# First attention: bias from skewed row slices, head norms inside the value projection, plain fp32 scores

## The chip, the cores and the metric

One core of a Trainium2 chip runs the kernel, one launch for the whole computation. The metric is the time of that launch on the device in microseconds (us). The engines are named as in the profile: PE (TensorE, matmuls), PEld (its weight loads), DVE (VectorE), ACT (ScalarE), POOL (GpSimd), SP (SyncE, which here only issues DMAs). Each runs its own instruction stream in program order and waits for the others by semaphores.

## What is computed

Two transformer blocks on 512 tokens of width 1024, in fp32. The change touches the first attention alone: 8 heads of width 64 whose queries and keys are normalised per head, with a bias that depends only on the distance of query and key, clipped at 128, and a mask by chunks of 64.

```python
def chunked_attention(q, k, v, q_gain, k_gain, rel_bias):
    q = rmsnorm(q.reshape(B, S, N_HEADS, HEAD_DIM), q_gain)
    k = rmsnorm(k.reshape(B, S, N_HEADS, HEAD_DIM), k_gain)
    ...
    rel_idx = jnp.clip(qpos - kpos, -REL_CLIP, REL_CLIP) + REL_CLIP
    bias = rel_bias.astype(jnp.float32)[:, rel_idx]
    ...
        s = jnp.einsum('bqhd,bkhd->bhqk', qb, kb).astype(jnp.float32) * scale + bias
        s = jnp.where(valid[None, None], s, NEG_INF)
        p = jax.nn.softmax(s, axis=-1)
        return jnp.einsum('bhqk,bkhd->bqhd', p.astype(vb.dtype), vb)

def hybrid_mixer(h, w_in, q_gain, k_gain, rel_bias, pool_w, pool_scale, w_out):
    proj = h @ w_in          # q, k, v, u: 512 columns each
    a = chunked_attention(q, k, v, q_gain, k_gain, rel_bias)
    p = multiscale_pool(u, pool_w, pool_scale)
    return jnp.concatenate([a, p], axis=-1) @ w_out
```

## The kernel before

Activations lie transposed (128 features on the partitions, 512 tokens along the row). A precise product is made of three products of the faster type fp32r, high by high, high by low and low by high part (`split3`, lines 357, 360, 361), so each weight block is cast by ACT (`split_hi`, L603) and its remainder taken by DVE (`split_lo`, L1123). SP fetches weight blocks of 512 KB into a ring of 4; a block's place is free when PE starts the block three ahead of it, and ACT and DVE prepare blocks 2 ahead of the one in use. Every engine's order is written out by hand.

The mixer of the first block runs as follows. `columns("qk", 8, ...)` makes eight tiles of queries and keys (head pair i in tile i); ACT squares each (`head_sq`), and `head_stat` sums the squares per head (L1985). `values("v", ...)` makes the value projection, k = 0 to 7, 12 products each; between them stand `head_stat` for the last pairs, `turn_rstd` (L1993, the inverse norms turned to rows) and `head_spread` (L2018, a row spread over 64 partitions). On the other side ACT takes the square root (L744) and casts the rows (L747), DVE takes the reciprocal (L1288) and the rows' remainder (L1290), then scales each tile (`qk_full`, L1302); ACT casts the result (L752) and DVE takes its remainder (L1294). Then `side_steps("u", ...)` makes the first tile of u.

The attention goes in 18 steps w; p = w // 4 is the head pair, q = w % 4 the query tile, so a step handles 128 queries against 128(q+1) keys for two heads c, called units 2w and 2w+1. In a step PE makes the scores (`a_scores`, units in partitions 0 to 63 and 64 to 127, output in banks 4 and 5), weighs values of a pair begun 5 steps ago (`a_weigh`, L2067), turns the probabilities of the step before (`a_turn`, L2080) and fills in products of u. DVE adds the bias and takes the minimum (`a_min`, L1319), and at w = 4, 9 and 14 empties a tile of u (`u_tile`, L1363), without which the next tile's products can't start; `pooled_lo` (L1358) stands ahead of it at w = 8. ACT takes the exponential (L770) and the copies L779 and L791.

The near part of the bias (where distance is not clipped, 192 or 256 columns) is made per head: ACT issues a DMA that reads the padded row from DRAM at 128 shifts (`toeplitz`, L726), PE multiplies it with a reversal matrix (`a_bias`, L2043 and L2044, bank 2), and ACT copies it out (L758, L759). Two heads are made before step 0, one each in steps 2, 3, 6, 7, 10 and 11. The order in which they stand there:

```python
            pe.wait_ge(acc_free, RES["v"] + TT)
            for h in range(2):
                a_bias(h)
            pe.wait_ge(qk_lo, 8)
```

## Time and profile before

| what | value |
|---|---|
| median of 3 runs | 1593.04 us |
| the three runs | 1593.31, 1587.33, 1593.04 us |
| profiled execution, own time | 1593.06 us |
| its span, first to last instruction | 1591.3 us |
| mean granted TensorE clock | 0.991 |
| PE busy | 1551.6 us (98%) |
| DVE, ACT, POOL busy | 760.0, 573.1, 79.1 us |
| chain that ended last | PE 90%, DVE 4%, ACT 2% |

The profile is of one execution. A row in order of time gives start, length, engine, line, operation, output<-input and in brackets how long the engine stood idle and who released it. Matmul lengths overlap, so what a matmul costs is read from the distance of two starts. In a row of a stretch, PEclk is the granted TensorE clock (1.00 is 2.4 GHz, 0.50 is 1.2 GHz).

### The profile page before, as it was taken

How to read it: one execution, taken by the hardware profiler on the slowest of the kernel's cores; microseconds unless marked ns; L12 is line 12 of the kernel's file. 1: busy time of each engine (PE TensorE's matmuls, PEld its weight loads, DVE VectorE, ACT ScalarE, POOL GpSimd, SP SyncE). 2: the span in 40 equal slices, each digit the busy share in tenths (PEclk: the TensorE clock that was granted, in tenths of full speed). 3: DMA queues.
4: the chain of work that ended last, by engine and by line, in shares of the span. 5: the costliest groups of instructions: out<-in, count | busy, mean ns of one | idle time of the engine just before them, and what ended most of it. 6: DMA issues, size and time to landing. Idle time of an engine off the chain costs nothing.

```text
span 1591.3 us, 19192 instructions
## 1 busy us (share of the span) xinstructions
PE 1551.6 (98%) x7150; PEld 1257.2 (79%) x7150; DVE 760.0 (48%) x1104; ACT 573.1 (36%) x941; POOL 79.1 (5%) x66
## 2 busy tenths in 40 slices
PE   8999999999989899999999999999998999999998
PEld 7888888878866688888888878777777888888886
DVE  5444422456365554444323465686644543244434
ACT  5222221234236442322212363446643343124322
POOL 0000000001013110000000051100000000000000
PEclk9999999999999999999999999999999999999999
DMA  6333333333221233333333333321131332233322
GB/s 189 95 92 100 98 94 97 101 101 110 78 63 41 66 106 93 97 100 92 97 102 93 96 103 90 110 80 41 49 137 41 93 93 105 93 93 92 102 97 93
DMA packets 246026, 147.66 MB, mean 93 GB/s; under 512 B 17472, under 2 KB 230096, under 8 KB 245840
## 3 DMA queue, kind: packets, MB, share of 16 engines
q1 hardware_dynamic: 232896, 141.58, 29.8%
q10 hardware_dynamic: 13072, 5.31, 1.3%
q8 instruction: 37, 0.61, 0.2%
q14 instruction: 21, 0.17, 0.0%
HBM read 142.66 MB, written 4.21 MB: 92 GB/s over the span
## 4 chain that ended last, share of the span: by engine, by line
PE 90%; DVE 4%; ACT 2%; issue 1%; DMA 1%; POOL 0%; SPq 0%; DVEq 0%; ACTq 0%; POOLq 0%
PE bank L357 29%; PE bank L361 28%; PE bank L360 28%; DVE w_low L1123 1%; ACT w_high L603 1%; PE bank L2266 1%; PE bank L2067 1%; PE bank L2383 1%; PE bank L2080 1%; DMA region_f<-in_x 0%; PE bank L1985 0%; DVE c_acc L1508 0%; DMA w_raw<-in_w_out 0%; DVE d_s L1489 0%; PE bank L2171 0%
## 5 line engine op out<-in xcount | busy, mean ns | idle before, releaser
L357 PE MATMUL bank<-region,w_high 128*128 128x512 f32 (+1 forms) x1484 | 586.1, 395 | 7.5 <-DVE region L1178 1.4
L361 PE MATMUL bank<-region,w_low 128*128 128x512 f32 (+1 forms) x1484 | 579.1, 390 | 0.0
L360 PE MATMUL bank<-region,w_high 128*128 128x512 f32 (+1 forms) x1484 | 579.1, 390 | 0.0
L1123 DVE TENSOR_TENSOR w_low<-w_raw,w_high 128x1024 fp32r<-128x1024 f32 (+1 forms) x259 | 335.7, 1303 | 147.8 <-ACT w_high L603 143.8
L603 ACT CAST w_high<-w_raw 128x1024 fp32r<-128x1024 f32 (+1 forms) x259 | 265.4, 1027 | 259.1 <-DMA w_raw<-in_ffn_w_down 106.9
L357 PEld LDWEIGHTS bank<-region,w_high 128*128 128x128 f32 (+1 forms) x1484 | 278.9, 188 | 71.1 <-DVE w_low L1123 5.9
L361 PEld LDWEIGHTS bank<-region,w_low 128*128 128x128 f32 (+1 forms) x1484 | 278.8, 188 | 60.2
L360 PEld LDWEIGHTS bank<-region,w_high 128*128 128x128 f32 (+1 forms) x1484 | 279.0, 188 | 57.6
L357 PE MATMUL bank<-w_high,region 128*128 128x512 f32 x416 | 166.1, 399 | 4.5 <-DVE w_low L1123 1.8
L361 PE MATMUL bank<-w_high,region 128*128 128x512 f32 x416 | 163.5, 393 | 0.0
L360 PE MATMUL bank<-w_low,region 128*128 128x512 f32 x416 | 163.4, 393 | 0.0
L657 ACT CAST region<-ff_t 128x512 f32 (+1 forms) x76 | 47.2, 621 | 207.1 <-DVE ff_t L1169 203.4
L1166 DVE TENSOR_TENSOR ff_u<-bank,rstd 128x512 f32<-128x512 f32 x44 | 30.4, 692 | 152.0 <-PE bank L361 152.0
L357 PEld LDWEIGHTS bank<-w_high,region 128*128 128x128 f32 x416 | 79.0, 190 | 23.1 <-DVE w_low L1123 2.7
L361 PEld LDWEIGHTS bank<-w_high,region 128*128 128x128 f32 x416 | 78.9, 190 | 17.0
L360 PEld LDWEIGHTS bank<-w_low,region 128*128 128x128 f32 x416 | 79.0, 190 | 15.7
L1178 DVE TENSOR_TENSOR region<-ff_t,region 128x512 f32 (+1 forms) x76 | 52.3, 688 | 52.0 <-ACT region L657 52.0
L1163 DVE TENSOR_TENSOR ff_z<-bank,rstd 128x512 f32<-128x512 f32 x44 | 30.4, 691 | 97.8 <-PE bank L361 89.7
L1199 DVE SCALAR_TENSOR_TENSOR x<-bank,x 128x512 f32<-128x512 f32 x24 | 16.6, 690 | 125.7 <-PE bank L361 125.6
L646 ACT ACTIVATE ff_s<-ff_z 128x512 f32<-128x512 f32 x44 | 27.9, 634 | 125.4 <-DVE ff_z L1163 125.3
L655 ACT ACTIVATE ff_t<-ff_z 128x512 f32<-128x512 f32 x32 | 20.3, 633 | 107.3 <-DVE ff_z L1176 107.3
L357 PE MATMUL bank<-f_rest,w_high 128*128 128x512 f32 x128 | 51.0, 399 | 0.0
(259 smaller groups left out, 1171.1 us busy)
## 6 DMA issues: line engine op xcount, KB each, us to landing
w_raw<-in_ffn_w_down SPq DMA_DIRECT2D x48, 512.0 KB, 4.0
w_raw<-in_ffn_w_gate SPq DMA_DIRECT2D x44, 512.0 KB, 3.7
w_raw<-in_ffn_w_up SPq DMA_DIRECT2D x44, 512.0 KB, 3.7
w_raw<-in_w_in SPq DMA_DIRECT2D x40, 512.0 KB, 3.8
w_raw<-in_w_up SPq DMA_DIRECT2D x32, 512.0 KB, 3.9
w_raw<-in_w_down SPq DMA_DIRECT2D x32, 512.0 KB, 3.2
w_raw<-in_w_out SPq DMA_DIRECT2D x16, 512.0 KB, 3.7
region_f<-in_x SPq DMA_DIRECT2D x4, 512.0 KB, 7.3
```

The costliest lines, as they stand in the source:

```text
L357: mm = pe.matmul(out, a_hi, b_hi, start=start, stop=False)
L360: pe.matmul(out, a_hi, b_lo, start=False, stop=False)
L361: return pe.matmul(out, a_lo, b_hi, start=False, stop=stop)
L603: last = act.copy(piece(w_high[b % RING]), piece(w_raw[b % RING]))
L646: act.activation(ff_s[:, j % 2, :], ff_z[:, j % 2, :], ACT.Silu).then_inc(s_ready, 1)
L655: act.activation(ff_t[:, j % 2, :], ff_z[:, j % 2, :], ACT.Square).then_inc(t_ready, 1)
L657: act.copy(dst[:, bass.ds(idx, 1), :] if it is not None else dst[:, idx, :], ff_t[:, j % 2, :]).then_inc(hid_hi, 1)
L1123: last = dve.tensor_tensor(piece(w_low[b % RING]), piece(w_raw[b % RING]), piece(w_high[b % RING]).bitcast(F32), ALU.subtract)
L1163: dve.tensor_tensor(ff_z[:, j % 2, :], bank[r % BANKS][:], rstd[:], ALU.mult).then_inc(z_ready, 1)
L1166: dve.tensor_tensor(ff_u[:, j % 2, :], bank[(r + 1) % BANKS][:], rstd[:], ALU.mult).then_inc(acc_free, 2)
L1178: dve.tensor_tensor(low_of(dst, place, idx, it), ff_t[:, j % 2, :], place.bitcast(F32), ALU.subtract).then_inc(hid_done, 1)
L1199: dve.scalar_tensor_tensor(x[:, n, :], acc[:], 0.5, x[:, n, :], ALU.mult, ALU.add).then_inc(acc_free, 1)
```

## The change

The near bias is no longer computed on PE. DVE writes the padded row reversed and negated (`rel_back`), ACT stores it to DRAM and copies all eight heads' rows 128 times over (`rel_rep_dram`, 128 x 12 KB) in the first FFN; `bias_load` then reads for each head two skewed slices (64 rows of 192 and of 256 elements) straight into `bias`, for heads 0 to 3 before the mixer, for 4 and 5 in step 4, for 6 and 7 in step 8. The constant parts of `bias` are set by DVE in the first FFN. The head norms' statistics, square root, turn and rows stand earlier in the value projection, among the weight blocks' casts. The scaled queries and keys stay fp32 (`over[1]`, the same memory as `part[1]`), without cast and remainder, and the scores are one fp32 matmul per unit.

```diff
@@ buffers
-        toep = sb("toep", [P, 2, 2, P])
-        rel_rows = sb("rel_rows", [HEADS, 384])
+        rel_rows = sb("rel_rows", [HEADS, N_REL])
+        rel_back = sb("rel_back", [HEADS, REL_ROW])
...
+        rel_rep_dram = nc.dram_tensor("rel_repeated_rows", [P, HEADS * REL_ROW], F32).ap()
@@ ACT: small loads in the first FFN, n is the tile of f1_dn0
                 if n == 0:
                     act.wait_ge(rel_padded, 1)
-                    act.dma_start(rel_pad_dram, rel_rows[:]).then_inc(rel_stored, 16)
+                    act.dma_start(rel_pad_dram, rel_back[:]).then_inc(rel_stored, 16)
+                if n == 1:
+                    act.wait_ge(rel_stored, 16)
+                    one = rel_pad_dram[0:1, 0:1].copy()
+                    act.dma_start(rel_rep_dram, bass.AP(one.tensor, one.offset, [[0, P], [1, HEADS * REL_ROW]])).then_inc(rel_repeated, 16)
@@ ACT: after the first FFN
-            act.wait_ge(rel_stored, 16)
-            for h in range(2):
-                toeplitz(h)
+            def bias_load(h):
+
+                if h >= 4:
+                    act.wait_ge(a_biased, 2 * TT * (h // 2 - 1))
+                for row0, width in ((0, 192), (64, 256)):
+                    at = REL_ROW * h + P - 1 - row0
+                    first = rel_rep_dram[row0:row0 + 1, at:at + 1].copy()
+                    skew = bass.AP(first.tensor, first.offset, [[HEADS * REL_ROW - 1, 64], [1, width]])
+                    act.dma_start(bias[row0:row0 + 64, h % 4, 256:256 + width], skew).then_inc(bias_in[h % 4], 16)
+            act.wait_ge(rel_repeated, 16)
+            act.wait_ge(bias_cleared, 1)
+            for h in range(4):
+                bias_load(h)
             act.wait_ge(lam_summed, 1)
             act.activation(lam_ex[:], bank[5][:, 0:2], ACT.Exp).then_inc(ev_hi, 1)
-            act.copy(head_select[:], const[:, C_HROW:C_HROW + 2 * S]).then_inc(select_made, 1)
             for i in range(8):
                 split_hi(BLK["qk"] + i + AHEAD)
                 if i == 0:
                     head("m1")()
+                if i == 3:
+                    act.copy(head_select[:], const[:, C_HROW:C_HROW + 2 * S]).then_inc(select_made, 1)
...
-            for i in range(3):
-                split_hi(BLK["v"] + i + AHEAD)
+            split_hi(BLK["v"] + AHEAD)
             act.wait_ge(h_stat, 8)
             act.activation(head_std[:], bank[4][:, 0:TT * 2 * HEADS], ACT.Sqrt, scale=1.0 / 64, bias=eps_col[:]).then_inc(h_std, 1)
+            split_hi(BLK["v"] + 1 + AHEAD)
             act.wait_ge(h_turned, 1)
             act.wait_ge(select_made, 2)
             act.copy(head_rows[0:2 * HEADS, :], bank[5][0:2 * HEADS, :]).then_inc(h_rows_hi, 1)
...
+            split_hi(BLK["v"] + 2 + AHEAD)
+            split_hi(BLK["v"] + 3 + AHEAD)
@@ ACT: step w of the attention
-                if w < 2:
-                    toeplitz(w + 2)
-                if q >= 2 and 2 * p + q < HEADS:
-                    bias_copy(2 * p + q)
-                    if 2 * p + q + 2 < HEADS:
-                        toeplitz(2 * p + q + 2)
+                if w in (4, 8):
+                    for h in (2 * p + 2, 2 * p + 3):
+                        bias_load(h)
@@ DVE: first FFN (pad_rows)
+                for s_ in range(4):
+                    link(dve.memset(bias[0:64, s_, 448:512], BIG))
+                    ins = dve.memset(bias[:, s_, 0:256], 0.0)
+                ins.then_inc(bias_cleared, 1)
@@ DVE: value projection
             for i in range(8):
-                if i == 2:
-                    split_lo(BLK["v"] + 3 + AHEAD)
+                if i in (2, 4):
+                    split_lo(BLK["v"] + 1 + i // 2 + AHEAD)
                 dve.wait_ge(h_bc, i + 1)
-                if i >= 2:
-                    dve.wait_ge(qk_lo, i - 1)
-                dve.scalar_tensor_tensor(qk_full[:, i % 2, :], qk_raw[:, i, :], qk_gain[:, i // 4:i // 4 + 1],
+                dve.scalar_tensor_tensor(over[1][:, i, :], qk_raw[:, i, :], qk_gain[:, i // 4:i // 4 + 1],
                                          bank[6 + i % 2][:], ALU.mult, ALU.mult).then_inc(qk_full_ready, 1)
-                if i > 0:
-                    qk_norm_lo(i - 1)
@@ DVE: a_min_of and the start of the attention
-                    dve.wait_ge(b_done, h + 1)
+                    dve.wait_ge(bias_in[h % 4], 32 * (h // 4 + 1))
...
-            for s_ in range(4):
-                link(dve.memset(bias[:, s_, 0:256], 0.0))
-                link(dve.memset(bias[0:64, s_, 448:512], BIG))
@@ PE
             def after_v(k):
-                if k == 1:
-                    for i in range(5, 8):
-                        head_stat(i)
+                for i in ((5,), (6, 7), (), (), (), (), (), ())[k]:
+                    head_stat(i)
+                if k == 2:
+                    turn_rstd(bank[5], 2 * HEADS, h_rec, h_turned)
                 if k == 3:
-                    turn_rstd(bank[5], 2 * HEADS, h_rec, h_turned)
                     pe.wait_ge(h_rows_lo, 1)
-                for i in ((), (), (), (0, 1), (2, 3), (4,), (5, 6), (7,))[k]:
+                for i in ((), (), (), (0, 1), (2, 3), (4, 5), (6, 7), ())[k]:
                     head_spread(i)
...
-                    split3(pe, bank[4 + c][:, 0:n], part[1][rows_, p, q * P:(q + 1) * P], part[1][rows_, 8 + p, q * P:(q + 1) * P],
-                           part[1][rows_, 4 + p, 0:n], part[1][rows_, 12 + p, 0:n], True, True).then_inc(a_score, 1)
+                    pe.matmul(bank[4 + c][:, 0:n], over[1][rows_, p, q * P:(q + 1) * P], over[1][rows_, 4 + p, 0:n],
+                              start=True, stop=True).then_inc(a_score, 1)
...
             pe.wait_ge(acc_free, RES["v"] + TT)
-            for h in range(2):
-                a_bias(h)
-            pe.wait_ge(qk_lo, 8)
+            pe.wait_ge(qk_full_ready, 8)
...
-                if q >= 2 and 2 * p + q < HEADS:
-                    a_bias(2 * p + q)
```

Where the instructions stand now. On PE in the value projection, the end of k=1 to the first spread, before:

```order
L1985 MATMUL bank<-const,head_sq 128x2 x12
...
L361 MATMUL bank<-w_high,region 128x512
L1993 MATMUL bank<-const,head_rstd 16x128 x4
L2018 MATMUL bank<-head_rows,head_select 128x512 x2
L357 MATMUL bank<-w_high,region 128x512
```

and of the changed kernel:

```order
L1970 MATMUL bank<-const,head_sq 128x2 x4
...
L1970 MATMUL bank<-const,head_sq 128x2 x8
...
L1978 MATMUL bank<-const,head_rstd 16x128 x4
L357 MATMUL bank<-w_high,region 128x512
...
L2003 MATMUL bank<-head_rows,head_select 128x512 x2
L357 MATMUL bank<-w_high,region 128x512
```

The turn (L1993, now L1978) and the first spread (L2018, now L2003) stood side by side and now have the 12 products of k=3 between them. On ACT in the same stretch, from the last square to the rows, before:

```order
L740 ACTIVATE head_sq<-region_f 128x512
L603 CAST w_high<-w_raw 128x1024 x3
L744 ACTIVATE head_std<-bank,eps_col 128x64
L747 CAST head_rows<-bank 16x512
L752 CAST region<-qk_full 128x512 x2
```

and of the changed kernel:

```order
L748 ACTIVATE head_sq<-region_f 128x512
L607 CAST w_high<-w_raw 128x1024
L751 ACTIVATE head_std<-bank,eps_col 128x64
L607 CAST w_high<-w_raw 128x1024
L755 CAST head_rows<-bank 16x512
L607 CAST w_high<-w_raw 128x1024 x2
```

Two of the three casts moved behind the square root, one of them behind the rows. On ACT in step 8 (its exponentials of 128 columns, the copy of turned probabilities, the cast of a pooled tile), before:

```order
L770 ACTIVATE a_p,a_sum<-a_s,a_min 128x128
L779 COPY region_f<-bank 128x4x128
L770 ACTIVATE a_p,a_sum<-a_s,a_min 128x128
L791 CAST region<-u_pad 128x512
L603 CAST w_high<-w_raw 128x512
```

and of the changed kernel:

```order
L764 ACTIVATE a_p,a_sum<-a_s,a_min 128x128
L773 COPY region_f<-bank 128x4x128
L764 ACTIVATE a_p,a_sum<-a_s,a_min 128x128
L732 DMA bias<-rel_repeated_rows 64x192
L732 DMA bias<-rel_repeated_rows 64x256
L732 DMA bias<-rel_repeated_rows 64x192
L732 DMA bias<-rel_repeated_rows 64x256
L785 CAST region<-u_pad 128x512
L607 CAST w_high<-w_raw 128x512
```

Four DMA issues now stand ahead of the cast of the pooled tile.

## Rows read from the trace of the kernel before

**Rows 1.** The page: its head and the busy time of TensorE (us, share, instructions).
```profile
span 1591.3 us, 19192 instructions
...
PE 1551.6 (98%) x7150; PEld 1257.2 (79%) x7150; DVE 760.0 (48%) x1104; ACT 573.1 (36%) x941; POOL 79.1 (5%) x66
```

**Rows 2.** PE in order of time, value projection (start, us, engine, line, op).
```profile
440.50 0.39 PE L361 MATMUL bank<-w_high,region 128*128 128x512 f32 x1
442.28 0.60 PE L1993 MATMUL bank<-const,head_rstd 128*16 128x128 f32 x4 [1.40 <-DVE head_rstd L1288]
444.27 1.22 PE L2018 MATMUL bank<-head_rows,head_select 128*128 128x512 f32 x2 [1.38 <-DVE head_rows L1290]
...
460.07 0.40 PE L357 MATMUL bank<-region,w_high 128*128 128x512 f32 x1
```

**Rows 3.** Chain that ended last, 432 to 446 us (start, us, what).
```profile
435.66 3.77 DMA w_raw<-in_w_in
...
439.45 1.06 ACT w_high L603
...
440.54 1.22 DVE w_low L1123
```

**Rows 4.** By stretches (length, PE, PEld, DVE, ACT, POOL, PEclk, DMA, GB/s).
```profile
446.00:448.00 2.00, 2.00 (x6) 1.52 (x6) 1.20 (x2) 1.12 (x2) 0.00 (x0) 0.50 0.35 99
```

**Rows 5.** In order of time, opening of the first attention: PE, then DVE, then ACT.
```profile
465.52 0.38 PE L2043 MATMUL bank<-const,toep 128*128 128x128 f32 x2
...
467.67 0.33 PE L357 MATMUL bank<-region 64*128 64x128 f32 x2
...
468.16 0.50 PE L357 MATMUL bank<-region,w_high 128*128 128x512 f32 x1
...
465.72 0.69 DVE L1363 TENSOR_TENSOR u_pad<-bank,rstd 128x512 f32<-128x512 f32 x1 [0.69 <-PE bank L361]
...
468.49 1.28 ACT L770 ACT_TABLE_LOAD   x1
```

**Rows 6.** PE in order of time, step 2 and the start of step 3.
```profile
473.59 0.39 PE L2043 MATMUL bank<-const,toep 128*128 128x128 f32 x2
...
473.96 0.47 PE L357 MATMUL bank<-region,w_high 128*128 128x512 f32 x1
...
475.98 0.50 PE L357 MATMUL bank<-region 64*128 64x512 f32 x1 [0.39 <-DVE a_min L1319]
```

**Rows 7.** PE in order of time, steps 7 and 8: scores, weighing (L2067), turns (L2080).
```profile
491.43 0.50 PE L357 MATMUL bank<-region 64*128 64x512 f32 x2
...
492.33 0.65 PE L2067 MATMUL bank<-region_f 128*64 128x256 f32 x4
492.92 0.87 PE L2080 MATMUL bank<-const,a_p 128*128 128x128 f32 x6
...
494.87 0.34 PE L357 MATMUL bank<-region 64*128 64x128 f32 x2
...
495.35 0.44 PE L2067 MATMUL bank<-region_f 128*64 128x128 f32 x4
495.72 1.09 PE L2080 MATMUL bank<-const,a_p 128*128 128x128 f32 x8
```

**Rows 8.** In order of time, steps 8 and 9: ACT, DVE, PE; then the issues of toep.
```profile
497.29 0.61 ACT L791 CAST region<-u_pad 128x512 fp32r<-128x512 f32 x1
...
499.14 0.68 DVE L1363 TENSOR_TENSOR u_pad<-bank,rstd 128x512 f32<-128x512 f32 x1
...
499.97 0.47 PE L357 MATMUL bank<-region,w_high 128*128 128x512 f32 x1 [0.53 <-DVE u_pad L1363]
...
L726 ACTq DMA_DIRECT2D toep<-rel_padded_rows x8: 326/326/574, 377.4 to 494.3; - x8
```

**Rows 9.** The page's DMA issues (KB each, median us to landing).
```profile
w_raw<-in_ffn_w_down SPq DMA_DIRECT2D x48, 512.0 KB, 4.0
...
x<-x_spill ACTq DMA_DIRECT2D x4, 512.0 KB, 5.6
```

64 lines of the change are left out of this document (16 added, 48 removed).

## The prediction

> **What bounds the kernel now.** I read the page first, then the chain of work that ended last, then TensorE's instructions in order of time wherever that chain leaves TensorE. The page says that PE is busy for 98% of the span [rows 1]: a microsecond is worth a microsecond only where PE stands still, runs at a lower clock, or does work that can go. The change touches four stretches: the value projection (about 427 to 460 us), the opening of the first attention (460 to 468), its 18 steps (to 530), and some DMA and VectorE work in the first FFN.
>
> In the value projection the reader is to see two standstills. The third product group's last product starts at 440.50; products follow each other every 0.227 us (24 of them between 460.07 and 465.52 [rows 2, 5]), so the next piece of PE work could start at 440.73. It starts at 442.28 (turning the inverse norms, which waited for the reciprocal), and the piece after it, the spread, at 444.27, after another 1.38 us of waiting [rows 2]. Who was late is in the chain: the cast L603 waited for a weight block whose DMA took until 439.45, and the square root, the reciprocal and the row split stand behind this cast and its remainder on their engines, though nothing in them needs that block [rows 3]. After the two standstills the granted clock is 0.50 of full, i.e. 1.2 GHz instead of 2.4, here for 446 to 448 us [rows 4].
>
> At the opening, the last weight product before the attention is followed at 465.52 by bias products; the first scores start at 467.67 and the next weight product at 468.16 [rows 5]. Between lie four bias products, two ACT evictions, and a wait for them.
>
> **The change, part by part.** The sum is made against the profiled execution: 1593.06 us, of which the span is 1591.3 [rows 1] and 1.76 lies outside; the median of the three runs is 1593.04, so both can be used alike.
>
> 1. *Head norms beside the value projection.* The statistics of head pairs 5 to 7 move ahead (one after k=0, two after k=1), the square root no longer stands behind the third and second cast, and the turn stands one group of 12 products (12 x 0.227 = 2.7 us) ahead of the spread. Followed through: statistics end about 434.9; square root about 435.3, reciprocal by 436.0; the group k=2 ends about 437.7, so the turn waits for nothing (1.7 us spare). Turn until 438.3; then ACT 0.6 and DVE 0.7 make the rows by about 439.7, and k=3 ends at 441.0 (1.3 us spare). No standstill is left, and so I expect no clock loss. From 440.73 to the start of u's first product at 460.07 pass 19.34 us. What must run there is one turn (0.60 [rows 2]), 48 products and 8 spreads, at 0.227 each: 12.7 us, together 13.3. Gain **6.0 us**. The late weight block (landing 439.45) is then cast after the rows and its remainder made between norms 1 and 2, about 444; PE needs it about 454. Cover gone, it would cost at most the old 3 us of waiting. The last block of the four lands about 446 and delays norm 4 to about 448.3; the spreads that need norms 4 and 5 come at 450.6.
>
> 2. *Opening of the attention.* The bias is in place long before; the two pairs of bias products and their wait go. From the end of u's first tile (T, 465.52 before) to the next weight product were 2.64 us. Now the first score unit starts at T; the second needs bank 5, which DVE empties (before: 465.72 plus 0.69 [rows 5], i.e. T+0.9), and takes about 0.25: T+1.2. Gain **1.4 us**. The table load of 1.28 us before the first exponential [rows 5] started ahead of its wait, so it is now paid long before.
>
> 3. *Six bias products pairs inside the steps.* Each is 0.37 us of PE (473.59 to 473.96 [rows 6]). The first saves nothing: right after it PE waited for DVE's a_min at 475.98 [rows 6], and would now wait 0.37 longer. Five count: 5 x 0.37 = **1.9 us** gained. The ACT evictions beside them go too, but PE does not wait for ACT there.
>
> 4. *Scores in plain fp32.* Six fp32r products of a pair of units become two fp32 ones. A pair before: 0.48 us at 128 columns (494.87 to 495.35), 0.90 at 512 (491.43 to 492.33) [rows 7]; in between 0.62 and 0.76 by a straight line, sum of four 2.76. The new form, 64 rows and 128 columns of the array in fp32, is not in the trace. The nearest rows are the weighing products L2067 (fp32, two halves of the array by columns): 0.37 at 128 (495.35 to 495.72), 0.59 at 256 (492.33 to 492.92) [rows 7], so 0.22 per 128 columns, i.e. 0.81 and 1.03 for the larger ones, sum 2.80. Four rounds: 4 x 0.04 = **0.2 us** lost. That slope is two units at once. The upper bound is one after the other: 0.44 per 128 columns, 4.4 a round, 6.6 lost in all; the lower bound is the issue-bound pair of 128 (0.37) carried to 256 too: 0.9 gained. I take 0.2, since the fp32r pairs, which share the array by rows as the new ones do, also grow by only 0.14 per 128 columns, less than six products in a row could.
>
> The Trainium skill, page "TensorE: Matmul & The Clock Gate", section "The mechanism", says that matmuls start and end strictly in program order. Two instructions a unit, unit after unit, could then overlap only by half (0.33 us per 128 columns instead of 0.22); the row of L2067 does not bear this out for column halves, and it becomes a rival below.
>
> 5. *Bias loads on ACT.* Sixteen DMAs instead of eight. One issue takes 0.33 us, at most 0.57 [rows 8]. The first eight (2.6 to 4.6 us in all, two of them were there before) stand ahead of the norm m1, for whose spread PE did not wait; the copy of head_select moves out of the same place: free, and at most 1 us if all take 0.57. Four in step 4 stand ahead of the cast of a weight block and push it 0.4 us; DVE still has its a_min ready before PE asks: free. Four in step 8 stand ahead of L791 (before at 497.29), behind which are, on DVE, L1358 and then L1363 at 499.14, for which PE already waited (0.53 us at 499.97) [rows 8]. A DMA is issued beside ACT's datapath as soon as the instruction ahead is handed over, about 0.9 us before L791 started; 4 x 0.33 = 1.3 us then end 0.45 after it: **0.5 us** lost (0 if they are issued sooner, 1.4 at 0.57 each).
>
> 6. *First FFN.* Eight short memsets of bias move to a place in the first FFN after which DVE waits for PE, and one DRAM-to-DRAM DMA of 128 x 12 KB = 1.5 MB. A weight block is fetched three blocks (3 x 24 x 0.227 = 16.3 us) before PE needs it; landing takes 4.0 [rows 9], cast and remainder 1.06 + 1.22 [rows 3]: 10 us spare. Alone, 1.5 MB at the weight rate is 12 us shared with the weights, which would roughly double a landing: free.
>
> 7. Units that wait for a slightly later a_min at 512 columns (steps 7, 11, 15): **0.1 us** lost.
>
> Sum: -6.0 - 1.4 - 1.9 + 0.2 + 0.5 + 0.1 = **-8.5 us**, 1593.06 - 8.5 = **1584.6 us**. Half a per cent, about what a measurement of this kernel can tell from no change, is 8.0 us: the bounds are 1585.1 and 1601.0. The forecast lies just beyond the lower one.
>
> **The rivals.**
>
> - *Program order* (0.13): pairs of scores overlap only by half, 0.33 per 128 columns, 3.3 a round against 2.76: 2.2 lost instead of 0.2, **1586.6**. For it: fp32 by row halves is not in the trace. Against it: both kinds of pair in rows 7. This is the page's rule from above.
> - *One after the other* (0.06): no overlap, 6.6 lost: **1591.0**.
> - *The clock falls elsewhere* (0.12): step 8's wait grows to about 1 us, and the opening has a new one of 0.7. The two waits that preceded the fall at 444 were 1.40 and 1.38, two within 3 us [rows 2]; the single waits elsewhere in this stage left it at full. A fall like that one cost about 14 x 0.227 = 3.2 of the 6.0 us (12 products and two spreads at half speed): **1587.8**.
> - *The change doesn't do what it says* (0.04): the norm chain is still late because the DVE or ACT order holds it behind another block. One of the two waits stays, with its clock loss: about 4.5 of 6.0 lost, **1589.1**.
> - *Slower* (0.04): the 1.5 MB broadcast starves the weight queue in the first FFN. Taken as three 512 KB reads and three writes at the slowest such row, 5.6 us [rows 9], it lasts 33.6 us, and if no weight packet passes meanwhile, PE stalls for what exceeds the 10 us spare: 23.5, **1608**. It decides nothing below 10 us of delay, and turns the sign at 18.5. Against it: the queues carry weights 30% of the time only, and small ACT DMAs beside them left landings at 4.0.
> - *More gained than forecast* (0.11): step 8 costs nothing, scores gain 0.9, the first bias pair counts: -10.5, **1582.5**.
>
> The Trainium skill, "DMA: Bandwidth & Descriptors", section "Queues, rings and completion order", says that a DMA engine takes turns between queues packet by packet. By that rule the weights keep half the rate and the slower case is out; no row here shows a large DMA beside the weights.
>
> **How the numbers follow.** The forecast, with 1.5 us on either side for landings and rounding, has 0.50. Its part below 1585.1 is about 0.35; with the better case and a little of the program-order case (the runs shown differ by up to 6 us among themselves) **faster** gets 0.50, **same** 0.46 and **slower** 0.04. The range goes from 1580.5, under the better case, to 1591.2, just over the serial scores; what is left out is the broadcast and some on either side where two cases meet or the run is a low or a high one.
>
> **What would show it.** Right: no PE wait before the turn or the first spread, clock 1.00 through 441 to 452, u's first product about 454.0, first scores about 459.5, the weight product after them 1.2 us on; pairs of scores of 1.0 us at 512 columns; a wait near 1 us for L1363's successor in step 9. Wrong: pairs of 1.3 or 1.7 us at 512 columns (the order and serial rivals); a clock under 1.00 between 460 and 515; a PE wait for w_low between 205 and 240 us, with landings of ffn_w_down over 14 us (the broadcast); a wait of ACT for the repeated rows near 377 us that moves the spread of m1 past 386.

## The result: 1581.0 us, and where the time went

Five runs of the changed kernel took 1578.67 to 1581.55 us, median **1580.97 us**. Five runs of the kernel before beside them took 1586.35 to 1593.31 us, median 1590.94. The ratio is **0.995, 95% interval 0.9931 to 0.9969**, a gain of 10 us. The forecast was 1584.6 us (1580.5 to 1591.2).

The profiled run of the changed kernel took 1578.67 us; the profile's page answers to [rows 1]:

```profile
span 1576.9 us, 19023 instructions
PE 1537.4 (97%) x7086; PEld 1244.6 (79%) x7086; DVE 754.3 (48%) x1096; ACT 563.2 (36%) x917; POOL 77.8 (5%) x66
```

The two profiled spans differ by 14.4 us, more than the medians do, since the one of before is among its longest runs and the one of after among its shortest. So I cut both executions at the same places in TensorE's work and compared the pieces. Each number is the difference between the starts of two rows of TensorE's timeline (first product of the value projection, first product of u, last of the four sum spreads, first and last product on f3_rest):

```text
stretch (us)                          before    after   difference
start to value projection             426.94   428.00    +1.06
value projection                       33.13    27.04    -6.09
attention, u to the 4th sum spread     68.95    67.87    -1.08
from there to the last FFN's f3_rest  704.06   700.30    -3.76
last FFN, products on f3_rest         264.74   260.24    -4.50
rest                                   93.5     93.5      0.0
```

Most of the fourth row (3.4 us of 3.76) is a clock fall that one of the two executions has and the other has not: the granted clock is 0.94 and 0.72 in 940 to 950 and 950 to 960 us before, and 1.00 in both after. The change touches nothing there.

**Value projection.** Against [rows 2] and [rows 4], TensorE's instructions in order of time (start, duration, then line, operation and tiles), and its busy time and granted clock in the stretch of 440 to 450 us:

```profile
439.08 0.60 PE L1978 MATMUL bank<-const,head_rstd 128*16 128x128 f32 x4
442.27 0.63 PE L2003 MATMUL bank<-head_rows,head_select 128*128 128x512 f32 x2
...
440.00:450.00 10.00, 10.00 (x45) 1.00 0.20 56
```

Neither the turn (439.08) nor the first spread (442.27) has a bracket, so TensorE waited for neither, and the clock stays at its upper level, 2.4 GHz, as it does from 430 to 440 and from 450 to 460 us. The gain is 6.09 us where the working says 6.0. It depends on the execution: two more kernels of experiments 1 to 3 have the code of before up to the last FFN, and their value projections take 31.77 and 32.54 us in place of 33.13, so against them the gain is 4.7 and 5.5 us.

**Opening and steps.** Against [rows 5], [rows 7] and [rows 8]:

```profile
460.57 0.49 PE L2031 MATMUL bank<-region_f 64*128 64x128 f32 x2
461.42 0.48 PE L2031 MATMUL bank<-region_f 64*128 64x128 f32 x2 [0.37 <-DVE u_pad L1351]
461.84 0.50 PE L357 MATMUL bank<-region,w_high 128*128 128x512 f32 x1
...
505.26 0.70 PE L2031 MATMUL bank<-region_f 64*128 64x256 f32 x4
505.89 1.08 PE L2042 MATMUL bank<-region_f 128*64 128x512 f32 x4
...
511.91 1.13 PE L2031 MATMUL bank<-region_f 64*128 64x512 f32 x4
512.97 0.65 PE L2042 MATMUL bank<-region_f 128*64 128x256 f32 x4
```

From the end of u's first tile (460.50, the last product's start plus 0.23) to the next weight product pass 1.34 us in place of 2.64. Each L2031 row is a score pair, and the next row's start is its end: 0.63 us at 256 columns and 1.06 at 512 here, and 0.42 at 128 (502.75 to 503.17) and 0.85 at 384 (509.68 to 510.53) beside them. In the kernel before, the pairs at 384 columns take 0.73 us, from the first of these starts to the second, and those at 256 0.56 (497.44 to 498.00):

```profile
502.56 0.45 PE L357 MATMUL bank<-region 64*128 64x384 f32 x2
503.29 0.87 PE L2067 MATMUL bank<-region_f 128*64 128x384 f32 x4
```

Two places in the steps of the changed kernel are worse than before. One is step 9, which answers to [rows 8]; first ACT, then DVE, then TensorE:

```profile
488.28 0.45 ACTq L732 DMA_DIRECT2D bias<-rel_repeated_rows  x1
...
489.42 1.25 ACTq L732 DMA_DIRECT2D bias<-rel_repeated_rows  x2
490.71 0.62 ACT L785 CAST region<-u_pad 128x512 fp32r<-128x512 f32 x1 [1.58 <-issue]
...
491.36 0.69 DVE L1346 TENSOR_TENSOR region<-u_pad,region 128x512 fp32r<-128x512 f32 x1 [2.08 <-ACT region L785]
491.97 0.69 DVE L1114 TENSOR_TENSOR w_low<-w_raw,w_high 128x512 fp32r<-128x512 f32 x1
492.57 0.68 DVE L1351 TENSOR_TENSOR u_pad<-bank,rstd 128x512 f32<-128x512 f32 x1
...
493.40 0.47 PE L357 MATMUL bank<-region,w_high 128*128 128x512 f32 x1 [2.14 <-DVE u_pad L1351]
```

Four issues of bias loads end at 490.67, the cast of u_pad behind them starts at 490.71, and its remainder, a weight remainder and u_pad's new tile follow one after the other on DVE. TensorE waits 2.14 us where it waited 0.53 [rows 8]. The other is step 15, in the rows of experiment 8.

### The profile page after: what moved, and what is told of

Read it like the earlier page. It is cut to its first block, busy times and chain, and to the rows that moved or that the text cites. A ratio compares the mean times of both kernels' runs of the same rounds, so it can differ in the third digit from the quotient of the medians.

```text
span 1576.9 us, 19023 instructions
## 1 busy us (share of the span) xinstructions
PE 1537.4 (97%) x7086; PEld 1244.6 (79%) x7086; DVE 754.3 (48%) x1096; ACT 563.2 (36%) x917; POOL 77.8 (5%) x66
## 4 chain that ended last, share of the span: by engine, by line
PE 90%; DVE 4%; ACT 2%; issue 1%; DMA 1%; ACTq 0%; POOL 0%; SPq 0%; DVEq 0%; POOLq 0%
PE bank L357 28%; PE bank L361 28%; PE bank L360 28%; DVE w_low L1114 1%; PE bank L2031 1%; ACT w_high L607 1%; PE bank L2236 1%; PE bank L2042 1%; PE bank L2055 1%; PE bank L2353 1%; DMA region_f<-in_x 0%; PE bank L1970 0%; DVE c_acc L1493 0%; DVE d_s L1474 0%; DMA w_raw<-in_w_out 0%
## 5 line engine op out<-in xcount | busy, mean ns | idle before, releaser
L357 PE MATMUL bank<-region,w_high 128*128 128x512 f32 (+1 forms) x1484 | 583.8, 393 | 9.2 <-DVE u_pad L1351 2.1
L357 PEld LDWEIGHTS bank<-region,w_high 128*128 128x128 f32 (+1 forms) x1484 | 278.0, 187 | 71.8 <-DVE w_low L1114 7.5
L357 PE MATMUL bank<-w_high,region 128*128 128x512 f32 x416 | 165.2, 397 | 4.4 <-DVE w_low L1114 1.7
L357 PEld LDWEIGHTS bank<-w_high,region 128*128 128x128 f32 x416 | 78.5, 189 | 22.8 <-DVE w_low L1114 2.5
L357 PE MATMUL bank<-f_rest,w_high 128*128 128x512 f32 x128 | 49.8, 389 | 0.0
```

The costliest lines, as they stand in the source:

```text
L357: mm = pe.matmul(out, a_hi, b_hi, start=start, stop=False)
```

## Experiments

Each kernel ran beside the kernel before on one chip; "ratio" is against that one, whose median was 1589.3 us beside experiments 1 to 4, 1587.5 beside 6 to 9 and 1587.6 beside 5 and 10 to 12. A wait or a start is read from the profiled execution.

### 1 to 3: the 4.5 us of the last FFN, which nothing in the change touches

In the last FFN, 384 products read their moving operand from f3_rest. Their rows, grouped by line (times, busy us, mean ns), in the kernel before:

```profile
L357 PE MATMUL bank<-f_rest,w_high 128*128 128x512 f32 x128 | 51.0, 399 | 0.0
```

and after the change:

```profile
L357 PE MATMUL bank<-f_rest,w_high 128*128 128x512 f32 x128 | 49.8, 389 | 0.0
```

The change shrinks the small tiles ahead of f3_rest (rel_rows 1536 to 1028 bytes per partition, rel_back 1536 more, toep 2048 less, and rounding to 32). By the declared sizes that moves f3_rest down by 992 bytes in its partition, from 32 past a multiple of 64 to a multiple of 64. Three kernels shift it without the change, together with the tiles that share or follow its place.

```diff
         with ExitStack() as s:
+            # an unused tile ahead of it: 8 floats (32 bytes), or 16 (64 bytes)
             ff_z = sb("ff_z", [P, 2, S], F32, s)
```

> The kernel before with one unused tile of 32 bytes per partition ahead of ff_z, so that ff_z and all that shares its space start at 203136-type addresses that 64 divides, where they started 32 bytes past such an address. Theory (address): the last feed-forward block reads its moving operand f3_rest from there, and twelve L357 groups take 8.16 us after the change and 8.32 us before; with 21 such groups the kernel before would gain 3.3 us by this pad alone (ratio 0.998), L357 on f_rest falling from a mean of 399 ns to 389 ns, with the stretches ahead of 1300 us unchanged. Rival (something else in the change, such as the order of the work or fewer instructions): the pad does nothing, 399 ns stays, ratio 1.000.

> The changed kernel with the same unused 32 bytes per partition ahead of ff_z, which puts f3_rest 32 bytes past a multiple of 64. Address theory: L357 on f_rest back to a mean of 399 ns, 3.3 us more than the changed kernel (about 1584.3 us if that one is at 1581.0, ratio to the kernel before 0.997). Rival: 389 ns and 1581.0 us stay, ratio 0.995.

> Control for the address: the kernel before with 64 unused bytes per partition ahead of ff_z. All tiles behind it move, by as much again as 32 bytes do, but f3_rest stays 32 bytes past a multiple of 64. Address theory: nothing, L357 on f_rest at 399 ns, ratio 1.000. Rival (any shift of the tiles changes it, or the bank that they fall in): 389 ns or another value.

The clean measure is the spacing inside the block, since the stretch as a whole also has a changing clock loss at its start. TensorE's timeline, the 17th and the 57th f3_rest product of line L357 (L358 where the padding adds a line). Before:

```profile
1256.39 0.40 PE L357 MATMUL bank<-f_rest,w_high 128*128 128x512 f32 x1
...
1311.86 0.40 PE L357 MATMUL bank<-f_rest,w_high 128*128 128x512 f32 x1
```

After, and the kernel before with 32 bytes of padding:

```profile
1245.00 0.39 PE L357 MATMUL bank<-f_rest,w_high 128*128 128x512 f32 x1
...
1299.40 0.39 PE L357 MATMUL bank<-f_rest,w_high 128*128 128x512 f32 x1
```

```profile
1251.57 0.39 PE L358 MATMUL bank<-f_rest,w_high 128*128 128x512 f32 x1
...
1305.97 0.39 PE L358 MATMUL bank<-f_rest,w_high 128*128 128x512 f32 x1
```

In the changed kernel with 32 bytes of padding they start at 1248.00 and 1303.46, in the kernel before with 64 at 1250.51 and 1305.98.

Between the two starts lie 240 products, 40 groups of three on f3_rest and as many on another tile; they take 55.47, 54.40, 54.40, 55.46 and 55.47 us. The spacing follows the place of f3_rest in all five kernels, whatever else they hold, and in the nine of the other experiments too (55.47 us in scores_alone, which has the place of before, 54.40 in the eight others), so it is the address. In both of its fast places f3_rest lies at a multiple of 128, in the slow ones 32 or 96 past one; a start 64 past one was not tried, so multiples of 64 and of 128 are not told apart. It costs 1.07 us over the 120 products, **0.0089 us for each 512-column product**, 3.4 us over 384. The whole-kernel times agree: before_pad32 1584.03 us (ratio 0.9973, interval 0.9961 to 0.9984), after_pad32 1585.16 (0.9984, 0.9972 to 0.9995), before_pad64 1588.16 (0.9997, 0.9982 to 1.0011).

### 4: the order of the head norms undone

```diff
# ACT (DVE alike, with remainders and the reciprocal)
-split_hi(BLK["v"] + AHEAD)
+for i in range(3):
+    split_hi(BLK["v"] + i + AHEAD)
 act.wait_ge(h_stat, 8)
 act.activation(head_std[:], ..., ACT.Sqrt, ...)
# PE, behind block k of the value projection
-for i in ((5,), (6, 7), (), (), (), (), (), ())[k]:
-    head_stat(i)
-if k == 2:
+if k == 1:
+    for i in range(5, 8):
+        head_stat(i)
+if k == 3:
     turn_rstd(bank[5], 2 * HEADS, h_rec, h_turned)
```

The copy of head_select goes back to its old place as well.

> The changed kernel with the order of the head norms as before: three casts of value weights ahead of the square root on ACT, three remainders ahead of the reciprocal on DVE, sums 5 to 7 together behind the second block and the turn behind the fourth. The plain fp32 scores and the bias by skewed loads stay, and no casts or remainders of q and k are made. Theory of the prediction: PE waits again ahead of the turn and of the spread (about 5 us together with the lower clock that follows), from the start of the value projection to the start of u0 33.1 us in place of 27.0, so 6.0 us more than the changed kernel (about 1587, ratio to before 0.998). Rival (the casts and remainders of q and k held the chain up too): only 3 to 4.5 us come back.

1587.52 us, ratio 0.9995 (0.9982 to 1.0009). The value projection takes 32.28 us in place of 27.04: 5.2 us come back. TensorE's timeline has waits again, and a clock row by stretches of 2 us has a fall in another place than before:

```profile
435.02 2.78 PE L1968 MATMUL bank<-const,head_sq 128*128 128x2 f32 x24
...
446.89 0.74 PE L2001 MATMUL bank<-head_rows,head_select 128*128 128x512 f32 x2 [1.38 <-DVE head_rows L1285]
...
454.78 0.50 PE L2001 MATMUL bank<-head_rows,head_select 128*128 128x512 f32 x1 [1.22 <-DVE region_f L1291]
...
438.00:440.00 2.00, 2.00 (x6) 1.56 (x5) 2.00 (x2) 0.58 (x1) 0.00 (x0) 0.52 0.23 54
440.00:442.00 2.00, 2.00 (x7) 1.59 (x6) 0.03 (x1) 0.00 (x0) 0.00 (x0) 0.63 0.69 208
```

(In the last two rows the clock is the number ahead of the last two.) The wait of 1.38 us ahead of the first spread is one of the two expected. The other, ahead of the turn, is missing, and one of 1.22 us for a late norm, which was not expected, stands at 454.78. And the clock is at 0.52 and 0.63 from 438 to 442 us, ahead of both waits, behind the 24 sum products of two columns each (L1968, 2.78 us). Since these slow products end later, the turn finds its reciprocal ready. This put the question of experiment 5.

### 5: only the sums of squares together again

```diff
-for i in ((5,), (6, 7), (), (), (), (), (), ())[k]:
+for i in ((), (5, 6, 7), (), (), (), (), (), ())[k]:
     head_stat(i)
```

> The changed kernel with the sums of squares 5 to 7 (24 products of two columns each, 2.78 us in one run) together behind the second block of the value projection, as in the kernel before, where the changed kernel has 8 behind the first and 16 behind the second; the rest of the new order stays. The clock of PE was granted at 0.5 to 0.6 for some microseconds behind these 24 in one kernel (438 to 442 us of norms_undone), ahead of any wait, and behind the waits in the kernel before (446 to 448 us). Theory 1 (a stretch of such small products is enough): the clock falls at 436 to 442 us and the value projection takes 28.5 to 30 us in place of 27.04, or a chain of ACT and DVE that is now late makes PE wait by up to 1.5 us as well. Theory 2 (only PE's idle time lowers the clock): it stays at 1.00 there, 27.0 to 27.5 us.

1582.13 us, ratio 0.9974 (0.996 to 0.9987). TensorE's timeline and its clock by 2 us:

```profile
433.11 2.78 PE L1970 MATMUL bank<-const,head_sq 128*128 128x2 f32 x24
436.98 0.63 PE L357 MATMUL bank<-w_high,region 128*128 128x512 f32 x1
...
440.18 0.60 PE L1978 MATMUL bank<-const,head_rstd 128*16 128x128 f32 x4
...
436.00:438.00 2.00, 2.00 (x6) 0.50 0.16 37
438.00:440.00 2.00, 2.00 (x8) 0.65 0.76 225
```

No row has a wait, the products behind the 24 thin ones run at half the clock, and the value projection takes 28.60 us in place of 27.04: 1.6 us, from leaving the 24 together in place of 8 and 16 with full products between. In the changed kernel the 16 together (434.52, 1.84 us) are followed by a clock of 1.00. So the clock can be at 1.2 GHz behind thin products though TensorE was never idle, as it is behind standing still in [rows 4].

It need not be. Six kernels have the 24 together, with one profile each. In before_pad32, norms_undone and this one the clock falls behind the sums; in the kernel before, before_pad64 and scores_alone it stays at 1.00 there and falls behind the waits. In the kernel before, behind its sums of 432.51 to 435.29:

```profile
436.00:438.00 2.00, 2.00 (x10) 1.63 (x9) 1.52 (x2) 0.08 (x1) 0.00 (x0) 1.00 0.51 140
```

Each of the six has exactly one fall in this stretch; none of the eight kernels with 8 and 16 has any. Which of the two places it takes differs by execution, and why is open.

### 6 and 7: the bias loads

The first eight, at the head of the q/k projection, and those of steps 4 and 8, each moved alone.

```diff
 for i in range(8):
     ...
     act.activation(head_sq[:, i % 2, :], qk_raw[:, i, :], ACT.Square)...
+    if 2 <= i < 6:
+        bias_load(i - 2)
```

> The changed kernel with the first eight bias loads issued two by two behind the squares 2 to 5 of the q/k projection, in place of all eight at its start. Theory (the eight issues, 0.45 to 0.62 us each, hold up ACT ahead of the mixer norm): PE's wait at the norm's spread falls from 0.50 us to about that of the kernel before, the first matmuls of the second block come 0.8 us sooner, and nothing new waits, 0.8 us less than the changed kernel (1580.2 if that one is at 1581.0). Rival (the norm's chain was late for another reason, such as x arriving 0.3 us later): less than 0.3 us.

1579.84 us, ratio 0.9954 (0.9938 to 0.997). The wait at the norm's spread, in the changed kernel

```profile
386.99 1.16 PE L1835 MATMUL bank<-const,r_col 128*128 128x128 f32 x8 [0.50 <-DVE r_col L1132]
```

is gone, and the spread starts at 385.63. The value projection starts at 426.53 us in place of 428.00. As starts vary from run to run, I compare groups: in seven profiles with all eight loads ahead it starts at 427.33 to 429.45, mean 428.1; in the three with the loads moved at 426.5 to 427.5, mean 426.9; in four with the old bias 426.6 to 427.9, mean 427.2. The eight issues cost about 0.9 us against the old bias, and 1.1 us come back when they move. They take 4.96 us (0.62 each), where the working had 0.33 to 0.57. The loads of toep in the kernel before show where most of the difference lies: the six that stand alone take 0.33 us each, but the first two, issued one behind the other, 0.41 and 0.57:

```profile
377.43 1.02 ACTq L726 DMA_DIRECT2D toep<-rel_padded_rows  x2
```

The first of four skewed loads takes 0.45 (488.28), those behind it 0.62. So a toep load right behind another costs 0.24 us more than one that stands alone, and the skewed shape costs 0.04 to 0.05 us more than toep in the same position; no skewed load stands alone here.

```diff
-if w in (4, 8):
-    for h in (2 * p + 2, 2 * p + 3):
-        bias_load(h)
 if w >= 5 and q == 1:
     a_spread_copy(p - 1)
 ...
 if w in (1, 4, 8, 12):
     split_hi(BLK["u"] + ...)
+if w in (4, 8):
+    for h in (2 * p + 2, 2 * p + 3):
+        bias_load(h)
```

> The changed kernel with the four bias loads of step 4 and the four of step 8 issued by ACT at the end of their step, behind the cast of u_pad and of the weights, in place of ahead of them. Theory (issues ahead of the cast delay it, then the remainder and u_pad on DVE, on which PE waits 2.14 us at step 9): that wait falls to about 0.5 us as in the kernel before, 1.6 us less than the changed kernel (1579.4 if that one is at 1581.0). Rival (the wait came from the loads' own time or from what DVE has to do, not from ACT's order): the wait stays near 2.1 us. Second rival: the issues now hold up the exponentials of steps 5 and 9, and a new wait of 0.5 to 2 us stands ahead of a turn there.

1579.67 us, ratio 0.9946 (0.9931 to 0.9961). ACT and then TensorE in its step 8 and 9:

```profile
488.50 0.60 ACT L785 CAST region<-u_pad 128x512 fp32r<-128x512 f32 x1
...
489.62 0.62 ACTq L732 DMA_DIRECT2D bias<-rel_repeated_rows  x1
...
491.47 0.51 ACT L764 ACTIVATE a_p<-a_s,a_min 128x256 f32<-128x256 f32 x1 [1.85 <-DVE a_min L1307]
...
491.17 0.47 PE L357 MATMUL bank<-region,w_high 128*128 128x512 f32 x1 [0.45 <-DVE u_pad L1351]
```

The cast goes first, the issues run beside the weight cast, and they are done 1.2 us before the next exponential is asked for. The wait is 0.45 us in place of 2.14: 1.7 us, the first theory's 1.6. Its loop has no wait that the changed one lacks.

### 8: the tail, DVE and POOL

In the changed kernel TensorE waits 2.19 us ahead of the turn of step 15, 1.36 us before. On DVE and POOL, first the changed kernel, then the one before:

```profile
513.35 1.68 DVE L1342 TENSOR_TENSOR region<-sq,region 128x512 fp32r<-128x512 f32 x1 [0.90 <-ACT region L795]
513.21 1.27 POOL L1794 TENSOR_TENSOR u_pad<-win,u_pad 128x512 f32<-128x512 f32 x1
516.99 1.28 PE L2055 MATMUL bank<-const,a_p 128*128 128x128 f32 x8 [2.19 <-ACT region_f L773]
```

```profile
520.39 0.69 DVE L1354 TENSOR_TENSOR region<-sq,region 128x512 fp32r<-128x512 f32 x1 [0.90 <-ACT region L801]
520.45 1.77 POOL L1809 TENSOR_TENSOR u_pad<-win,u_pad 128x512 f32<-128x512 f32 x1
523.04 1.28 PE L2080 MATMUL bank<-const,a_p 128*128 128x128 f32 x8 [1.36 <-ACT region_f L779]
```

The same two operations meet in both kernels. When POOL's subtraction starts 0.14 us ahead, DVE's remainder takes 1.68 us; when DVE is 0.06 us ahead, it takes 0.69 us and POOL's takes 1.77 in place of 1.27. Behind DVE's stands a_min of step 15, for which the exponential and the copy ahead of the turn wait; behind POOL's, nobody that is late.

```diff
+if j == 3:
+    pool.wait_ge(a_olo, 2)
 pool.tensor_tensor(u_pad[:, g, PAD:], src[:, PAD:], u_pad[:, g, PAD:], ALU.subtract)...
```

> The changed kernel in which POOL's last subtraction (L1794, last window) waits until DVE has stored the remainder of the second head pair (L1342). In the changed kernel that remainder takes 1.68 us, starting 0.14 us behind POOL's, where 0.69 us is its time without POOL beside it; a_min of step 15 is later by it, and PE waits 2.19 us for the turn's copy. Theory (the two operations exclude each other): L1342 0.69 us, the wait 1.2 us, 1.0 us less at the start of out1. Rival (the 1.68 us has another cause, such as a wait inside the instruction for ACT): 1.68 us and the wait stay.

1578.33 us, ratio 0.9944 (0.9926 to 0.9961).

```profile
513.11 0.69 DVE L1342 TENSOR_TENSOR region<-sq,region 128x512 fp32r<-128x512 f32 x1 [0.90 <-ACT region L795]
513.96 1.28 POOL L1796 TENSOR_TENSOR u_pad<-win,u_pad 128x512 f32<-128x512 f32 x1 [1.06 <-DVE region L1342]
515.77 1.28 PE L2057 MATMUL bank<-const,a_p 128*128 128x128 f32 x8 [1.21 <-ACT region_f L773]
```

The remainder takes 0.69 us, the wait 1.21. The attention from u to the fourth sum spread takes 65.24 us in place of 67.87; 1.0 us of that is the wait, the other 1.6 us a clock fall at 510 to 530 us (0.95 and 0.88 in the changed kernel) that this run does not have. after_pad32, which has the wait and like this run no fall, takes 66.22 us: against it the gain is 0.98 us, and the fall is not shown to be the wait's doing. Of the seven kernels with a wait of 2.18 or 2.19 us six have a fall here; of the seven with 1.21 to 1.37, three (the kernel before, best_fp32 and best_split). From the third to the fourth sum spread it takes 11.5 or 11.6 us with the short wait and no fall, 12.6 with the long one and no fall, and 1.5 to 2.6 us more with a fall.

The Trainium skill, "GPSIMD Engine Reference", section "1. Specifications", in its table, says that POOL shares its SBUF interfaces with VectorE and contends with DVE instructions that have two SBUF inputs. Both operations here have two, and the rows agree: one holds the other up in full.

### 9 and 10: the scores alone, and everything but the scores

```diff
# scores_alone, in the kernel before; scores_split is the reverse, in the changed one
-act.copy(part[1][:, i, :], qk_full[:, i % 2, :])        # and the remainder on DVE
-dve.scalar_tensor_tensor(qk_full[:, i % 2, :], ...)
+dve.scalar_tensor_tensor(over[1][:, i, :], ...)
-split3(pe, bank[4 + c][:, 0:n], ...)
+pe.matmul(bank[4 + c][:, 0:n], over[1][rows_, p, ...], over[1][rows_, 4 + p, 0:n], ...)
```

> The kernel before with the scores alone changed: q and k stay plain fp32, no cast and no remainder of them is made, and each score tile is one fp32 product in place of three. The order of the head norms and the bias by toep and products stay. By the prediction's estimates a pair of scores goes from 0.48, 0.62, 0.76, 0.90 us to 0.37 to 0.43, 0.59 to 0.63, 0.81 to 0.85, 1.03 to 1.06 us: over the sixteen steps 0.2 to 0.9 us more. The opening no longer waits for the last remainder (0.4 to 1.4 us less), and casts no longer hold up the spreads of the head norms (0 to 1 us less). Sum: between 2.2 us less and 0.5 us more than the kernel before; by two products in strict order it would be 1.7 to 2 us more in the steps, and pairs at 512 columns at 1.7 us.

1593.29 us, ratio **1.0034 (1.002 to 1.0049)**: slower than the kernel before, outside the range expected. The opening gains only 0.13 us, because the wait for the bias copies stays (0.87 us at 466.71). And the tail has the collision of experiment 8, which the kernel before escapes, with the wait of 2.19 us at the turn (524.41):

```profile
520.77 1.68 DVE L1340 TENSOR_TENSOR region<-sq,region 128x512 fp32r<-128x512 f32 x1 [0.90 <-ACT region L796]
520.63 1.27 POOL L1795 TENSOR_TENSOR u_pad<-win,u_pad 128x512 f32<-128x512 f32 x1
```

From u to the third sum spread it takes 56.31 us, before 55.75: 0.6 us more. With the 0.83 us at the turn that is 1.4 of 5.8 us (3.2 to 7.8 by the interval). Another 1.6 us may be the fall of experiment 8, which this profile has too (clock 0.54 and 0.60 from 526 to 530 us) and two of the three profiles with the old scores have not. The rest, and whether that fall comes in every execution, stays open.

> The changed kernel with the scores alone as before: q and k are cast and get a remainder again (their fp32 form stands in the two halves of sq, two at a time), and each score tile is three products. The order of the head norms and the skewed bias loads stay. Theory A (plain fp32 scores cost more on PE than they save, and it is their few tenths per step that put POOL's last subtraction 0.14 us ahead of DVE's remainder of the second head pair): from the start of u to the third sum spread 0.3 to 0.6 us less than the changed kernel's 53.62 us; the wait of 2.19 us at the turn of step 15 back at about 1.36 us; value projection within 0.3 us of 27.04 us, since the last cast and remainder are done 5 us ahead of the first scores; 1.0 to 3 us less than the changed kernel in all (1578 to 1580). Theory B (the missing casts and remainders are what lets the head norms go beside the value projection): PE waits for the spreads again, the value projection 1 us longer or more, and the opening 0.4 to 1.4 us longer; no gain or a loss against the changed kernel.

1581.27 us, ratio 0.9953 (0.9938 to 0.9968), the same as the changed kernel, so neither theory holds alone. From u to the third sum spread it takes 54.51 us where theory A had 53.0 to 53.3: this profile has a clock fall behind the wait of step 9 (2.21 us, then 0.50 from 494 to 496), the kind of fall that the prediction named as a rival, which the changed kernel's profile has not. The value projection takes 28.23 us, 1.2 more than 27.04, with a wait of 0.89 us for a norm: theory B's effect, since every norm on DVE (0.75 us) now has a remainder (0.68) behind it, 2.9 us for two, while two spreads come every 3.2 us and two weight remainders of 1.23 stand between. The tail is A's: DVE 0.08 us ahead of POOL, 0.69 us long, and 1.37 us of wait at the turn (517.29):

```profile
514.63 0.69 DVE L1356 TENSOR_TENSOR region<-sq,region 128x512 fp32r<-128x512 f32 x1 [0.90 <-ACT region L800]
514.71 1.75 POOL L1808 TENSOR_TENSOR u_pad<-win,u_pad 128x512 f32<-128x512 f32 x1
```

### 11 and 12: all repairs together, with each form of the scores

Both have the edits of experiments 6 to 8.

> The changed kernel with the three edits that each removed one wait: the first eight bias loads behind squares 2 to 5, those of steps 4 and 8 at the end of their step, POOL's last subtraction behind DVE's remainder. If the waits are independent: 0.8, 1.6 and 1.0 us less, 3.4 us in all, 1577.5 us if the changed kernel is at 1581.0, and up to 1.6 us more where PE's clock no longer falls in the tail. Rival (they share a cover, a wait that goes brings another forward): 2 us or less.

> The same three edits, with the scores of scores_split (three products of casts and remainders). By theory A 0.3 to 0.9 us less than best_fp32, about 1576.8 us; the wait at step 15's turn 1.2 to 1.4 us in both, so that the scores' own cost on PE is what differs. By theory B the same as or slower than best_fp32.

best_fp32 took **1577.14 us**, ratio 0.9937 (0.9916 to 0.9958); best_split 1576.74 us, 0.994 (0.9917 to 0.9963). Both medians are about 4 us under the changed kernel's 1581.0, but the intervals of the ratios overlap. The profiles say it more sharply: with plain fp32 the fourth sum spread comes at 518.79 us in place of 522.91, 4.1 us sooner with one clock fall in the tail of both, and the waits at step 9 and at the turn are 0.45 and 1.21 us. The repairs add up, to the expected 3.4 us and somewhat more. The pair also gives the price of the fp32 scores without a collision: from u to the third sum spread 51.71 us with plain fp32 and 51.08 us with three products, 0.6 us for fp32, and 1.2 us back in the value projection (27.04 against 28.21). On the chip the two are the same.

## Why the prediction was right, and where it was not

1. *Head norms*: -6.0 predicted, -6.1 found, 5.2 taken back by undoing the order. That the two standstills go is as written; that the size agrees so well is part luck. The working priced the clock loss (3.2 us) from one execution, in which the clock was low for about twice as long as in the profiles of before_pad32 and before_pad64; against those the gain is 4.7 and 5.5. The working also laid the clock loss on the two standstills; experiment 5 shows a loss of 1.6 us with no standstill, from the 24 sums together. The regrouping of the sums was named there as a step of the chain only. And 1.2 us of the 6.1 need the absence of the casts and remainders of q and k, which the working put under the scores, not here.
2. *Opening*: -1.4 predicted, -1.30 found.
3. *Bias products in the steps*, with 4 and 7: -1.9 + 0.2 + 0.1. To step 8 the changed kernel gains 1.9 us (from 5.0 + 1.3 = 6.3 us ahead at the opening to 8.2), though the fp32 scores are inside it, which cost 0.6 us over three of the four rounds by experiments 11 and 12; steps 10 and 11 give 0.6 more. So the pairs of products gave about 0.5 us each, not five times 0.37: from the turn to the next weight product step 7 takes 0.63 us (485.17 to 485.80) in place of 1.07 (492.92 to 493.99), 0.44 for one pair. And the first pair, which the working wrote off, counted: step 2 has 0.41 us in that place (466.67 to 467.08) in place of 0.86. The wait that it was to lengthen shows only in part, in the score pair of step 3, 1.54 us long (468.69 to 470.23) where others at 512 columns take 1.06.
4. *Scores*: 0.42, 0.63, 0.85, 1.06 us for a pair, where 0.37, 0.59, 0.81, 1.03 were estimated from L2067: 0.21 per 128 columns. A single fp32 product of 128 columns on all rows costs 0.20 (L1850, four of them from 386.09 to 386.89 in the kernel before), so the two units run side by side. Program order (0.33) and one after the other (0.44) fall. The loss is larger than the 0.2 predicted, though: the old pairs at 256 and 384 columns were put at 0.62 and 0.76 by a straight line where their rows say 0.56 and 0.73, and the new ones take 0.03 to 0.05 more each than estimated. By these rows a round goes from 2.67 to 2.96 us, 1.2 over four; experiments 11 and 12 found 0.6 over three. By the rule quoted from the Trainium skill, "TensorE: Matmul & The Clock Gate", section "The mechanism", starts and ends keep program order; the rows show that this leaves two row halves a full overlap, and it was my reading of it that halved the overlap.
5. *Bias loads*: +0.5 predicted for step 8, +1.6 found; up to 1 for the first eight taken as free, 0.9 found. The failed step is the price of an issue: 0.33 us, the median of the toep loads, most of which stood alone, where skewed loads in a row take 0.62. The upper end, 0.57, was a toep load behind another; it gives 1.4 us for step 8, near the 1.6 found. The spread of m1 at 386.99 is past the 386 that was named as a sign of trouble, but for the issues and not for a wait on the repeated rows. The place and the mechanism (a late cast, then L1346 and L1351 on DVE) were as written.
6. *First FFN*: the broadcast is in the trace as a DMA share of 0.49 in place of 0.38 from 200 to 250 us, with TensorE busy for all 50 us. Free, as predicted.
7. *Not in the working*: the collision of DVE and POOL (0.8 us of wait), and the address of f3_rest (-3.4 us).

Summed over the two profiles up to the fourth sum spread: +1.1 (start) - 6.1 - 1.3 - 2.5 (steps without step 8) + 1.6 (step 8) + 1.1 (tail) = **-6.1 us**, where the working had -8.5. What the working had too little of, the later start, the issues of step 8 and the collision (3.3 us), outweighs 0.9 us that the steps gave beyond it. The address brings 3.4 us more: -9.5, and the medians differ by 10.0. So the forecast came near because losses and a gain that it did not have nearly cancel: luck. And the -6.1 holds for these two executions. In the two other profiles with the code of before the fourth sum spread comes at 525.72 and 527.70 us in place of 529.02, in after_pad32 at 521.95 in place of 522.91; the means of the three and of the two differ by about 5 us. What the change is worth without the address is less sure: 1.5 to 7.6 us by taking 3.4 from the interval of its ratio, 0.8 to 4.4 us by after_pad32's own interval.

What rests on one profile each: the clock falls. From 940 us on, in work that no kernel here changes, all fourteen profiles have one near 1075 us, eleven one near 1225 and four one near 945 (the lowest clock over 10 us is 0.57). The stretch from the fourth sum spread to the last FFN takes 700.3 to 704.1 us by them.

## What to carry to other kernels

Price an issue of a DMA by how it stands, alone or behind another, and put it behind whatever a waiting engine needs from that queue. A kernel that is this full gains from side effects as much as from the change: compare a stretch that the change does not touch, and when its spacing differs, look at where its tiles now lie. Two elementwise operations on DVE and POOL that read two SBUF tiles each need an order; a tenth of a microsecond in the phase decides which of them pays.

## What the hardware showed that I had not expected

- The moving operand's address: products of 512 columns with f3_rest at a multiple of 128 bytes against 32 or 96 past one, 54.40 against 55.47 us for 240 products of which 120 read it. That is 0.0089 us each, about 4% of the 0.227 us between two products.
- TensorE's clock fell to 0.50 (1.2 GHz) behind 24 products of two columns each, with no idle time shown, in three of six profiles; in the other three it fell behind waits instead. With 8 and 16 of them, apart, it stayed at 1.00 in all eight.
- DVE 1.68 us in place of 0.69 behind a POOL subtraction that started 0.14 us sooner; POOL 1.77 in place of 1.27 the other way round.
- An ACT issue of a 64-row skewed load: 0.45 us for the first, 0.62 for those right behind it; of toep, 0.33 alone and 0.57 right behind another.
- Two fp32 products on different halves of the rows took 0.21 us per 128 columns together, one on all rows 0.20.
